# Two transformer blocks in float32: the 16-bit splits of the gated rows move from VectorE to ScalarE, and tails and hooks are put in another order

## The reference

```python
def rms_norm(x, g):
    y = x * lax.rsqrt(jnp.mean(x * x, axis=-1, keepdims=True) + 1e-6)
    return y * g

def swiglu_ffn(h, w_gate, w_up, w_down):      # 1024 -> 2816 -> 1024
    return (jax.nn.silu(h @ w_gate) * (h @ w_up)) @ w_down

x = x + 0.5 * rms_norm(swiglu_ffn(rms_norm(x, g_pre), w_gate, w_up, w_down), g_post)   # second block: without 0.5
```

## Time and profile before

| | |
|---|---|
| runs | 2031.08, 2034.59, 2035.2; median 2034.59 |
| profiled execution | 2030.87, span from first to last instruction 2029.1 |
| TensorE clock granted | 0.999 over the span |
| busy: TensorE, VectorE, ScalarE | 1990.8, 1649.4, 1298.4 |
| DMA engines, mean | 194 GB/s |
| ScalarE `high` from raw tiles | 340 instructions, 643.5 busy |
| VectorE `weight_low` from raw tiles | 336 instructions, 766.4 busy |
| ScalarE joins | 132 instructions, 92.9 busy |

### The profile page before, as it was taken

One profiled execution on the slowest core, in us unless ns is written; L12 is line 12 of the kernel. 1 busy time (PEld: TensorE's weight loads), 2 busy tenths in 40 slices (PEclk: granted clock), 3 DMA queues, 4 the chain that ended last, 5 costly groups with the idle time before them and its releaser, 6 DMA issues.

```text
span 2029.1 us, 24329 instructions
## 1 busy us (share of the span) xinstructions
PE 1990.8 (98%) x9370; PEld 1626.0 (80%) x9370; DVE 1649.4 (81%) x1958; ACT 1298.4 (64%) x1588; POOL 0.2 (0%) x4
## 2 busy tenths in 40 slices
PE   8999999999999999999999999999999999999998
PEld 6787887888877777887888878788888788888886
DVE  6888899778887888899778887976688879667887
ACT  6656657665666666667565576756665767566655
POOL 0000000000000000000000000000000000000000
PEclk9999999999999999999999999999999999999999
DMA  8765764557667675764557666654567575446673
GB/s 262 226 212 178 217 193 144 182 183 223 207 211 231 197 227 162 238 187 145 187 182 223 205 204 182 201 164 156 182 202 222 188 216 184 160 150 192 214 219 119
DMA packets 326835, 394.54 MB, mean 194 GB/s; under 512 B 123824, under 2 KB 210496, under 8 KB 326720
## 3 DMA queue, kind: packets, MB, share of 16 engines
q1 hardware_dynamic: 322624, 381.94, 60.5%
q10 hardware_dynamic: 4096, 11.05, 1.5%
HBM read 365.66 MB, written 1.05 MB: 181 GB/s over the span
## 4 chain that ended last, share of the span: by engine, by line
PE 74%; DVE 12%; ACT 5%; DMA 4%; issue 3%; SPq 1%; DVEq 0%; ACTq 0%
PE ps L741 57%; PE ps L878 9%; DVE w_lo L2133 4%; DMA scratch<-scratch 2%; ACT scratch L1537 2%; PE ps L812 1%; ACT w_hi L1430 1%; DVE scratch L2566 1%; SPq L572 1%; DMA raw<-in_ffn_w_up 1%; PE ps L1370 1%; PE ps L1351 1%; DVE scratch L2292 1%; DVE scratch L2218 1%; DVE form_lo L2133 1%
## 5 line engine op out<-in xcount | busy, mean ns | idle before, releaser
L2133 DVE TENSOR_TENSOR w_lo<-raw,w_hi 128x2048 fp32r<-128x2048 f32 x336 | 766.4, 2288 | 105.7 <-ACT w_hi L1430 104.1
L1430 ACT ACTIVATE w_hi<-raw 128x2048 fp32r<-128x2048 f32 (+2 forms) x340 | 643.5, 1897 | 302.4 <-PE ps L741 123.4
L741 PE MATMUL ps<-w_hi,hT_hi 128*128 128x512 f32 x1616 | 638.9, 395 | 9.1 <-DVE hT_lo L2224 9.1
L741 PE MATMUL ps<-w_lo,hT_hi 128*128 128x512 f32 x1616 | 630.5, 390 | 0.0
L741 PE MATMUL ps<-w_hi,hT_lo 128*128 128x512 f32 x1616 | 606.7, 390 | 0.0
L741 PEld LDWEIGHTS ps<-w_hi,hT_hi 128*128 128x128 f32 x1616 | 304.1, 188 | 77.7 <-issue 17.0
L741 PEld LDWEIGHTS ps<-w_hi,hT_lo 128*128 128x128 f32 x1616 | 303.7, 188 | 64.3
L741 PEld LDWEIGHTS ps<-w_lo,hT_hi 128*128 128x128 f32 x1616 | 304.4, 188 | 59.9
L741 PE MATMUL ps<-w_hi,bT_hi 128*128 128x512 f32 x608 | 239.9, 395 | 2.0 <-DVE bT_lo L2224 1.8
L741 PE MATMUL ps<-w_hi,bT_lo 128*128 128x512 f32 x608 | 237.0, 390 | 0.0
L741 PE MATMUL ps<-w_lo,bT_hi 128*128 128x512 f32 x608 | 236.9, 390 | 0.0
(11 more groups left out here) (340 smaller groups left out, 2186.3 us busy)
## 6 DMA issues: line engine op xcount, KB each, us to landing
raw<-in_w_in SPq DMA_DIRECT2D x160, 512.0 KB, 4.7
raw<-in_ffn_w_down SPq DMA_DIRECT2D x88, 512.0 KB, 4.3
raw<-in_ffn_w_gate SPq DMA_DIRECT2D x86, 512.0 KB, 4.2
raw<-in_ffn_w_up SPq DMA_DIRECT2D x86, 512.0 KB, 5.0
raw<-in_w_gate SPq DMA_DIRECT2D x44, 512.0 KB, 4.0
raw<-in_w_up SPq DMA_DIRECT2D x44, 512.0 KB, 4.9
raw<-in_w_down SPq DMA_DIRECT2D x44, 512.0 KB, 4.5
raw<-in_w_out SPq DMA_DIRECT2D x32, 512.0 KB, 4.1
```

The costliest lines, as they stand in the source:

```text
L741: mm = nc.tensor.matmul(bank(t, half), act[:, tiles[i], t * P:(t + 1) * P], w, start=start and (i, n) == steps[0], stop=stop and (i, n) == ...
L1430: nc.scalar.activation(dst, src, ACT.Copy).then_inc(high_ready, 1)
L2133: V.tensor_tensor(lo, src, flat(hi), ALU.subtract).then_inc(low_ready, 1)
```

## The change

ScalarE makes the splits (`part`, `pair_part`), each as two copies, one for each 128 rows; VectorE's are gone. On ScalarE a split stands behind the Silu of its chunk: behind one more high part for chunks 0 to 2 and 6 (directly behind `high` for chunk 1), before the last high part of chunks 3 and 7, at the end of a pair for its two chunks. In the tail, Silu and split of chunk 10 come before the join of chunk 9, and on VectorE the gating of chunk 10 before the low part of chunk 9. The loads of gain and constants (FFN 1) and of the memory (FFN 3) are started just before the first pair, the constants and angles are computed within chunk 6, `memory_std` runs after chunk 7 with a new wait in `t4` of the second pair, and `memory_rows` runs in the tail.

```diff
 # ScalarE, ffn
+            def part(c):
+                act.wait_ge(hid_ready, f * NCHUNK + (c + 1))
+                src = pairbuf[:, 512:1024].bitcast(U16).rearrange("p (t n b) -> p t b n", t=TT, b=2)
+                for t in range(TT):
+                    apart = nc.scalar.activation(halves[:, t, :, :], src[:, t, :, :], ACT.Copy)
+                apart.then_inc(halves_ready, 1)
+
+            def pair_part(c, which):
+                act.wait_ge(hid_ready, f * NCHUNK + (c + which + 1))
+                src = pair_hid[:, :, FC * which:FC * which + FC].bitcast(U16).rearrange("p t (n b) -> p t b n", b=2)
+                dst = second_halves if which else halves
+                for t in range(TT):
+                    apart = nc.scalar.activation(dst[:, t, :, :], src[:, t, :, :], ACT.Copy)
+                apart.then_inc(halves_ready, 1)
...
                 silu(L, k + 1, c)                        # chunk
                 if ahead:
+                    part(c)
                     form_high(c + 1, 2)
                 else:
                     high(L, k + 2 + AHEAD)
+                    part(c)
...
                     high(L, k + 5)                       # chunk_behind
+                    part(c)
                     high(L, k + 6)
...
                 nc.scalar.activation(pair_hid[:, 1, :], sum_3, ACT.Silu, scale=rstd_in[:, 1:2]).then_inc(silu_ready, 1)
+                for which in range(2):                   # pair
+                    pair_part(c, which)
...
             silu(L, k0 + 1, 0, 0)
             high(L, k0 + 1 + AHEAD)
+            part(0)
             high(L, k0 + 2 + AHEAD)
...
             high(L, k0 + 4 + AHEAD)
+            part(1)
...
-                if c in PAIRS:
-                    pair(k0 + AT["p", c, 1], c)
-                    continue
-                if memory_here(L, n) and c == 2:
+                if memory_here(L, n) and c == PAIRS[0]:
                     memory_load()
-                (chunk_behind if c - 2 in PAIRS else chunk)(k0 + AT["gu", c, 0], c)
-                if L.sub0 + j == 0 and c == 2:
+                if L.sub0 + j == 0 and c == PAIRS[0]:
                     gain(post_g, 0, 1, post_loaded)
...
+                if c in PAIRS:
+                    pair(k0 + AT["p", c, 1], c)
+                    continue
+                (chunk_behind if c - 2 in PAIRS else chunk)(k0 + AT["gu", c, 0], c)
...
-                if memory_here(L, n) and c == 6:
+                if memory_here(L, n) and c == 7:
                     memory_std(L.l)
...
                 high(L, end - 1)                         # tail
                 hidden(c - 2)
                 high(L, end)
-                hidden(c - 1, second_hi)
                 act.wait_ge(halves_ready, L.turns(n, c - 1))
                 silu(L, end - 3, c, 4)
+                part(c)
+                hidden(c - 1, second_hi)
 # VectorE, ffn
-            def part(c):
-                dve.wait_ge(hid_ready, f * NCHUNK + (c + 1))
-                V.tensor_copy(halves, pairbuf[:, 512:1024].bitcast(U16).rearrange("p (t n b) -> p t b n", t=TT, b=2)).then_inc(
-                    halves_ready, 1)
...
                 b21 = landed(c, 2)                       # t4
+                if memory_here(L, n) and c == PAIRS[-1]:
+                    dve.wait_ge(*after("memory_std", "sum1", L.l))
...
+            def first_constants():
+                dve.wait_ge(const_loaded, 16 * 4)
...
+                rope_angles()
+
             def chunk_behind(k, c):
                 ahead = c + 1 in PAIRS
                 join(c - 2)
                 hidden_low(c - 2)
                 weight_low(L, k + 3)
+                if L.sub0 + j == 0:
+                    first_constants()
                 join(c - 1)
                 hidden_low(c - 1, second_hi, second_lo)
...
                 hidden_low(c - 2)                        # tail
                 weight_low(L, end - 1)
+                hidden(c, 4)
                 join(c - 1)
                 hidden_low(c - 1, second_hi, second_lo)
                 weight_low(L, end)
-                hidden(c, 4)
-                part(c)
...
             weight_low(L, end - 2 + AHEAD)
+            if memory_here(L, n):
+                memory_rows(L.l)
             join(c)
             hidden_low(c, hT_hi[:, 2:4, :], hT_lo[:, 2:4, :])
```

More of the change, by code:

```diff
@@ L62 @@
 JOIN_ON_ACT = True
-HOOK = 6
 TAIL_PAIR = NCHUNK - 3 in PAIRS
@@ L2300, in pair_sum @@
                 V.tensor_tensor(dst, a, b, ALU.add).then_inc(*done("forms", f"{step}_{c}", f))
[L2302 to L2305, removed]
             def low_form(c, number):
@@ L2341, in pair @@
                                            ALU.mult).then_inc(hid_ready, 1)
-                    pair_part(c, which)
                     weight_low(L, k + 9 + which)
@@ L2361, in chunk @@
                 hidden(c)
-                part(c)
                 if not ahead:
                     weight_low(L, k + 2 + AHEAD)
+            def first_constants():
+                dve.wait_ge(const_loaded, 16 * 4)
+                V.tensor_copy(sb_ident[:, :], ident).then_inc(*done("start", "ident"))
+                V.tensor_copy(sb_tri[:, :], konst("tri_ge")).then_inc(*done("start", "tri"))
+                V.tensor_copy(sb_bar[:, :], konst("sb_neg")).then_inc(*done("start", "bar"))
+                rope_angles()
             def chunk_behind(k, c):
@@ L2383, in ffn @@
             hidden(0, 0)
-            part(0)
             weight_low(L, k0 + 1 + AHEAD)
@@ L2399, in ffn @@
             hidden(1)
-            part(1)
             if PAIRS[0] == 3:
@@ L2412, in ffn @@
                 (chunk_behind if c - 2 in PAIRS else chunk)(k0 + AT["gu", c, 0], c)
[L2413 to L2420, removed]
             end, c = k0 + U_FFN - 1, NCHUNK - 1
```

## The result

The changed kernel takes 2051.87 us, median of 4 runs (2049.46 to 2053.79); the kernel before took 2032.84 beside it (4 runs, 2030.64 to 2035.2). The ratio is 1.0094, 95% interval 1.0081 to 1.0107: slower by 0.9%, 19 us. The profiled execution of the changed kernel took 2049.46, its span is 2047.7; before it was 2030.87 and 2029.1.

A forecast was written before the change was run, and what follows sets the result against it. TensorE, busy 98% of the span, was taken to bound the kernel. Terms summing to +20.7 us on the profiled 2030.9 gave 2051.6, rounded to 2051; forecast range 2046 to 2062 (chance 0.50), with 0.19 outside 2029 to 2063.

The forecast's parts named there:

- A: Starts of the FFN passes: the split delays the first down product, 1.2 us each in FFN 1, 2 and 6; +4.0 us.
- signs of being wrong: Splits well under 1.4 us for two, no wait in the first pairs of FFN 1 and 3, or the tails' waits vanishing.
- B: Inside the pairs of FFN 1, 3, 4 and 6: TensorE's waits from VectorE's lateness go; -5.6 us.
- E: Computations moved in FFN 1 (constants, angles) and FFN 3 (memory rows' normalisations and squares): +2.2 and +0.3, together +2.5 us.
- C: Down products inside pairs: later split halves delay them, 1.0 us in second pairs except FFN 3, 0.3 in four first pairs; +6.2 us.
- D: First pairs of FFN 1 and 3: loads moved ahead delay down(3)'s load, waits of 6.0 and 4.9 us; +10.9 us.
- the sharing rival: Queues divide the DMA engines, so down(3) waits 2.2 us in FFN 1 and 3; 2045 us in all, chance 0.22.
- the line: First pairs of FFN 1 and 3: transfers land in order of issue, whichever queue issued; down(3) waits 6.0 and 4.9 us.
- F: Tails of the passes: the wait moves from the tenth down to the ninth, FFN 3 loses 2.4 us; +2.7 us in sum.

## Why the prediction was right, and where its terms were not

The direction, the time (2051 against 2051.87) and the main causes came out. The sum of its terms, 20.7, met a span difference of 18.6, but partly by luck: terms that were off in opposite directions offset each other.

- **The split's price.** 1.4 for two copies, measured 1.14. The reading of ScalarE's rows at the starts (no idle time, so that the split adds to the path) was right, and so were the places: FFN 1, 2 and 6 wait, 3 and 5 as before, 4 not. A: +2.3 for +4.0; most of the miss is this price (three times 0.26, and the 0.2 each of FFN 3 and 5). Of the signs of being wrong, a split well under 1.4 came out in part; the first pairs do wait, and the tails' waits did not vanish.
- **B** held: -5.1 for -5.6 (without the wait treated in E). The waits stood in FFN 1, 3 and 6; FFN 4, which the prediction also names, had none. The moves alone leave 1.2 of them, the splits alone 2.5, so both parts of the reason count, the moves more.
- **C** held in size, not in its parts: the first pairs cost 0.19 to 0.99, 2.0 in sum for 1.2 (and 1.20 and 1.08 in FFN 1 and 3, seen only once the loads were out of the way), the second pairs 0.28 to 1.36, 4.5 in sum for 5.0. A `down(4)` in FFN 6 (0.84) was not foreseen, and 0.63 of it stays with the splits on VectorE; of the other nine none stays.
- **D** was right in the places and in what stands behind the load, and too large: 8.2 for 10.9, of which, in this kernel, 5.9 is the loads' and the rest C's. Landing came 10.5 and 10.3 after the first load's issue; less the 6.2 of the prediction that leaves 4.3 and 4.1, against waits of 4.17 and 3.98. I had taken 11 to 12 from transfers issued 3 to 6 places behind. In size the waits lie between the sharing rival's 2.2 and the forecast's 6.0 and 4.9; what speaks for the line is that engine time was not divided until the load's own queue had its transposes through.
- **E** was right in sum. In FFN 3 the 3.48 is VectorE's fourth form, waiting 4.09 for ScalarE's squares:

```profile
757.62 2.29 DVE L2311 TENSOR_TENSOR scratch<-raw,scratch 128x2048 f32<-128x2048 f32 x1 [4.09 <-ACT scratch L1880]
```

- **F** is the term that was mis-sized most: -1.1 for +2.7. The wait did move from the tenth down to the ninth, and the tenth has none, as worked out. But I had 1.6 at the ninth; it is 0.97 (1.14 in FFN 1), since the split is 0.26 shorter and chunk 10's gating ends 3.0 before the product is due and not 2.6. The chain in FFN 2, with the join right behind the split:

```profile
604.60 1.15 ACT L1543 ACTIVATE scratch<-scratch 128x512 uint16<-128x512 uint16 x2 [1.22 <-DVE scratch L2241]
605.66 1.40 ACT L1536 ACTIVATE scratch<-scratch 128x512 uint16<-128x512 uint16 x2
607.08 0.63 ACT L1556 ACTIVATE form_lo<-scratch 128x512 fp32r<-128x512 f32 x1
```

  So the tails gain 0.43 to 0.44 in FFN 2, 4, 5 and 6, where the prediction had +0.2 and +0.1, and 0.85 in FFN 1 for its 0.35. In FFN 3, where the normalisations stand before the last low half, the tail costs 1.5 more than before, not 2.4.
- **The clock** was missing. The prediction counted each wait at its length. The kernel before had one wait with slow products behind it (2.0, in FFN 1's tail), and I did not look there. The terms were 6.6 too large in sum (20.7 for some 14.1), and the 4.6 of the clock filled most of that. That is why 2051 came so close to 2051.87, and it was luck.

## What to carry to other kernels

Work moved to an engine that is idle on the average costs its whole duration where that engine's chain runs without a gap into the bounding engine, and nothing where its result is wanted much later: the same split cost 17 us over 66 places and, in another order, nothing over 24 of them. Before a transfer is moved, look at the DMA share behind the new place and at which load is due next: here its delay grew with the bytes put ahead, and was less than their time at 350 GB/s. And a wait of TensorE is to be priced with the slow products behind it: one of 4 us cost up to 7.

## What was not expected of the hardware

The cost of a long wait. Behind TensorE's waits of 2.9 us and more, 16 in all these traces after the first 20 us, 6 to 14 products ran at the lower level of the clock in all but one case, 1.3 to 2.9 us in sum. Behind shorter waits it differs from trace to trace: 7 slow products after one of 1.99 in the kernel before, none after one of 1.97 in the changed kernel, and none after the 2.70 in the kernel before. So two executions with like waits can differ by the 1.4 us of such a place.

The 16-bit copy that reads with a stride is cheaper on ScalarE here than the one that writes with it: two of 512 values take 1.14 (L1543) against 1.40 (the join, L1536), so the nearest row was not the price.
